# The index lookup of the top-k stage: both POOL subtractions of a head released by DVE's last index operation, which stands behind a weight split

## The reference, cut to what matters

```python
q = (xf @ wq).reshape(T, PEER_HEADS, 2, PEER_KEY_DIM // 2)
s1 = jnp.einsum('thd,kd->thk', q[:, :, 0], kf[0])
s2 = jnp.einsum('thd,kd->thk', q[:, :, 1], kf[1])
v1, i1 = lax.top_k(s1, PEER_TOPK)
v2, i2 = lax.top_k(s2, PEER_TOPK)
cand = (v1[..., :, None] + v2[..., None, :]).reshape(T, PEER_HEADS, PEER_TOPK * PEER_TOPK)
sc, ci = lax.top_k(cand, PEER_TOPK)
e1 = jnp.take_along_axis(i1, ci // PEER_TOPK, axis=-1)
e2 = jnp.take_along_axis(i2, ci % PEER_TOPK, axis=-1)
idx = e1 * PEER_N_KEYS + e2
g = jax.nn.softmax(sc, axis=-1)
```

## Time and profile before

| what | value |
| --- | --- |
| median of three runs | 3645.09 us |
| the profiled execution, its own time | 3633.96 us |
| its span | 3632.2 us |
| PE busy | 3337.1 us (92%) |
| DVE busy | 2583.1 us (71%) |
| ACT busy | 1226.2 us (34%) |
| POOL busy | 942.2 us (26%) |
| mean granted TensorE clock | 0.966 |
| route, first layer | about 440 to 715 us of the span |
| route, second layer | about 2250 to 2525 us |

### The profile page before, as it was taken

The page is one execution under the profiler, slowest core; times in us unless marked ns, Lnnn a source line. Parts: engine busy times, 40 slices in busy tenths (PEclk is TensorE's granted clock), DMA queues, the critical chain, the costliest instruction groups (busy, mean ns, idle before and its releaser), DMA issues. The chain is left out here.

```text
span 3632.2 us, 49494 instructions
## 1 busy us (share of the span) xinstructions
PE 3337.1 (92%) x17238; PEld 2880.9 (79%) x17238; DVE 2583.1 (71%) x5173; ACT 1226.2 (34%) x1704; POOL 942.2 (26%) x648
## 2 busy tenths in 40 slices
PE   7899899798899999999788997998988999999996
PEld 6755589788799999988677555897888999999885
DVE  2364479899688866678723654798996887766786
ACT  2244333333333333333222443333433333333332
POOL 0211001211155544333202110012111554343332
PEclk9999999999899999999999998999999999999998
DMA  9310024456799988789593001244668999887895
GB/s 268 84 42 1 25 83 136 166 220 253 279 344 360 337 277 281 260 291 355 198 261 100 11 1 37 82 139 163 236 233 307 358 355 325 280 275 246 316 352 185
DMA packets 326377, 773.84 MB, mean 213 GB/s; under 512 B 48686, under 2 KB 203822, under 8 KB 291918
## 3 DMA queue, kind: packets, MB, share of 16 engines
q1 hardware_dynamic: 252494, 503.46, 40.3%
q0 software_dynamic: 73728, 268.47, 20.6%
HBM read 689.02 MB, written 90.70 MB: 215 GB/s over the span
## 5 line engine op out<-in xcount | busy, mean ns | idle before, releaser
L219 PE MATMUL o_bank<-v_hi,w_hi 128*128 128x512 f32 x1536 | 599.0, 390 | 12.0 <-DVE w_lo L1426 12.0
L221 PE MATMUL o_bank<-v_hi,w_lo 128*128 128x512 f32 x1536 | 600.0, 391 | 0.0
L220 PE MATMUL o_bank<-v_lo,w_hi 128*128 128x512 f32 x1536 | 599.9, 391 | 0.0
L156 POOL DMA_INDIRECT g_ring<-in_peer_v,g_idx x256 | 398.0, 1555 | 659.4 <-DVE x_sb L174 615.6
L156 POOL DMA_INDIRECT g_ring<-in_peer_u,g_idx x256 | 332.7, 1300 | 727.0 <-DVE g_ring L166 682.6
L1411 DVE TENSOR_TENSOR v_lo<-v_raw,v_hi 128x2048 fp32r<-128x2048 f32 x128 | 293.2, 2290 | 215.5 <-ACT v_hi L1352 215.3
L219 PE MATMUL h_bank<-x_hi,ws_hi 128*128 128x384 f32 x1152 | 387.1, 336 | 4.5 <-PEq L1093 4.5
L221 PE MATMUL h_bank<-x_hi,ws_lo 128*128 128x384 f32 x1152 | 387.0, 336 | 0.0
L220 PE MATMUL h_bank<-x_lo,ws_hi 128*128 128x384 f32 x1152 | 386.6, 336 | 0.0
L1352 ACT CAST v_hi<-v_raw 128x2048 fp32r<-128x2048 f32 x128 | 244.8, 1913 | 387.5 <-PE o_bank L221 349.5
L166 DVE SCALAR_TENSOR_TENSOR g_ring<-g_ring,x_sb 128x1024 f32<-128x1024 f32 x256 | 307.4, 1219 | 81.9 <-DMA g_ring<-in_peer_u,g_idx 81.7
(11 more groups left out here) (181 smaller groups left out, 6208.3 us busy)
## 6 DMA issues: line engine op xcount, KB each, us to landing
ws_raw<-in_uT SPq DMA_DIRECT2D x128, 1024.0 KB
v_raw<-in_peer_v SPq DMA_DIRECT2D x128, 1024.0 KB
gates_T<-gate_stage SPq DMA_DIRECT2D x12, 4096.0 KB, 15.2
g_raw<-gates_T SPq DMA_DIRECT2D x128, 384.0 KB
w_raw<-in_w_in SPq DMA_DIRECT2D x24, 1024.0 KB, 7.6
ws_raw<-hidden_T SPq DMA_DIRECT2D x56, 384.0 KB
ws_raw<-in_peer_wq SPq DMA_DIRECT2D x16, 1024.0 KB
hidden_T<-r_hid SPq DMA_DIRECT2D x32, 384.0 KB, 6.1
```

The lines of the kernel that those rows point to most:

```text
L156: nc.gpsimd.indirect_dma_start(out=tail.ring[n % RING][:, :], out_offset=None, in_=table.rearrange("l e d -> (l e) d"), in_offset=bass.Ind ...
L219: nc.tensor.matmul(out, lh, rh, start=start, stop=False)
L220: nc.tensor.matmul(out, lh, rl, start=False, stop=False)
L221: return nc.tensor.matmul(out, ll, rh, start=False, stop=stop)
```

## The change

DVE's `ab[0]` (L983) no longer raises `placed`; the following step waits on DVE's own chain instead. Split "keys" moves ahead of the last index operation (L991 after, L990 before), which alone raises `placed`, once per head. Both of POOL's subtractions wait for that one increment.

```diff
                 ab = abf[j % 2]
-                nc.vector.scalar_tensor_tensor(ab[:, 0, :, :], shf[:, 1, :, :], -12.0 * RANK, shf[:, 0, :, :],
-                                               ALU.add, ALU.max).then_inc(placed, 1)
-                dve.wait_ge(placed, 2 * j + 1)
+                chain.done(nc.vector.scalar_tensor_tensor(ab[:, 0, :, :], shf[:, 1, :, :], -12.0 * RANK,
+                                                          shf[:, 0, :, :], ALU.add, ALU.max))
+                chain.wait()
                 for f in range(2):
                     chain.done(nc.vector.scalar_tensor_tensor(lin[:, f, :, :], ab[:, 0, :, :], -16.0 + 12.0 * f,
                                                               shf[:, 2, :, :], ALU.mult, ALU.add))
+                after("keys")
                 chain.wait()
                 nc.vector.scalar_tensor_tensor(ab[:, 1, :, :], lin[:, 1, :, :], -48.0 * RANK, lin[:, 0, :, :],
                                                ALU.add, ALU.max).then_inc(placed, 1)
-                after("keys")
...
                 for f in range(2):
-                    pool.wait_ge(placed, 2 * j + f + 1)
+                    pool.wait_ge(placed, j + 1)
                     if j >= 1:
                         pool.wait_ge(looked, 2 * (j - 1) + f + 1)
```

## The result

The changed kernel takes 3621.23 us (median of 7 runs, 3615.86 to 3626.43); the kernel before, in the same comparison, 3641.96 us (7 runs). The ratio is 0.9943, 95% interval 0.9931 to 0.9955: 20.7 us or 0.57% faster. Over all comparisons of this study the change has a mean of 3621.1 us (24 runs) and the kernel before 3640.6 us (87 runs), a gain of 19.5 us, plus or minus 1.8 (95%). The forecast was a gain of 14.4 us, and its range ended 1.5 us above the measured time. The profiled execution of the change took 3615.86 us, its span is 3614.1 us.

The account below looks back on a forecast made before the run. DVE's own time was taken to bound route's heads 3 to 7. Two layers at 7.2 us make 14.4 us, and 3645.09 less that gives 3630.7 us; range 3622.7 to 3640.

Parts of the forecast that it names:

- What bounds route, and the port: Route: DVE's own time sets heads 3 to 7; L987 stands for POOL's subtraction, 1.96 us against 0.22.
- the heads' part: Route, heads 3 to 7: a "keys" head saves 1.86 us of DVE; period near 26.4 us instead of 27.84.
- The rival by which the scan stands: Scan beside POOL's subtractions: a head pays 3.9 us and saves 1.86, giving 3665.5 us; chance 0.05.
- ACT's part as the new limit: Route, "keys" splits wait for ACT's high part; it takes back 1.8 of 9.3 us, head 7 7.52 earlier.
- K: Start of a "keys" split in route; the next head's "half" was to start at K + 12.98.
- The end of the stage: End of route: L1006 stands, goes between POOL's two subtractions and ends 7.3 us earlier; the stage ends 7.2 us earlier.
- the rival of one piece: End of route: POOL runs both subtractions without a gap, 5.4 us a layer instead of 7.2, 3634.3 us; chance 0.15.
- The 0.15 us that I charged to L1017: End of route: the first L1017, due at 701.07, stands 0.15 us until POOL's second subtraction ends.
- I see nothing in gates that would take it back: Gates stage, after route: it begins with the barrier and keeps route's gain of 7.2 us a layer.
- all other stages the same: Stages outside route: no change in length, while route is shorter by 7 us in each layer.
- The sum's base: Whole kernel: the runs' median, 3645.09 us, 11.1 above the profiled execution, from which 14.4 us was taken.
- the range's lower end: Whole kernel: 3622.7 us, from all of DVE's saving (3626.7) and 4 us of spread of medians below.

Follow-up runs that it names:

- the joint release alone: The change with the "keys" split put back behind the last index operation, both POOL subtractions still released by L990: 3626.56 us, ratio 0.9969; again 3627.03 us.
- the moved split alone: The kernel before with the "keys" split ahead of the last index operation, each subtraction released by its own index operation as before: 3635.55 us, ratio 0.999.
- softmax-ahead kernel: The change with head 7's L1004 and L1006 in front of `ab[0]` and the last lookup ahead of the products: 3623.59 and 3625.26 us.

## Why the prediction was wrong

**What bounds route, and the port: right.** L987 fell to 0.22 us, MAX8 and FIND_INDEX8 stayed, and the resource that DVE's two-input operations and POOL's subtractions exclude each other from was the whole reason for the heads' part: the joint release alone brings a head from 27.84 to 26.17 us, the moved split alone to 27.72, both together to 26.29. What the moved split adds lies at the end of the stage, where it leaves one operation standing instead of two. The rival by which the scan stands is out, also with twice the work on POOL.

**ACT's part as the new limit: right for the change, with small errors in size.** "Half" of head 3 starts at 574.92, K + 12.98 to the digit. K of head 7 came 7.76 us earlier counted from head 2's split (139.21 to 131.45 us), forecast 7.52: five heads take 131.45 us and not 131.69.

**The end of the stage: right.** L1006 went between the two subtractions, and the rival of one piece is out; why the one that waits gets its turn there no run shows. The 0.15 us that I charged to L1017 was not paid (it started at 700.19, as POOL ended). With the two small errors a layer gives 7.7 us, not 7.2, 1.0 us in all.

**The step that failed is the one that closed the account at the end of route**: "I see nothing in gates that would take it back", and "all other stages the same". Everything outside of route was put at 0 us; the runs show 4.1 us of gain there (19.5 less 15.4, plus or minus 1.8). I had looked for something that takes the gain back and not for something that adds to it. Gates can add: the experiment that put 1.4 us back at the end of route made its two gates stages 2 us longer, with no later stretch at a granted clock of 1.00. But between the kernel before and the change the gates stages differ by only 0.9 us in the mean, since two of the six of the kernel before are short too; that is 1.8 us of the 4.1, and not clear of their scatter. The difference in project and attend (1.3 us a layer) is smaller than their scatter from profile to profile (431.4 to 440.9 us), and no experiment was aimed at it. So the cause of the 4 us is shown in part at most, and stays open for the rest.

**The sum's base was the second error.** I carried the difference of the three runs shown over to the forecast; their median, 3645.1, lies 4.5 us above the mean of 87 runs, which puts the forecast that much too high. With the better base, 3640.6, the same 14.4 us would have given 3626. The forecast of 3630.7 was 9.5 us too high: 4.5 from the base, 1.0 from route and 4.1 from the other stages. And the range's lower end took the highest gain of route alone with 4 us of scatter, so that a gain of route as forecast, plus a few us from outside, fell out of it.

What stays open as well: whether it is PE's pause itself, or when gates starts against something else, that decides the clock. The softmax-ahead kernel has a still shorter pause, 2.5 us, and gates stages in between, 262.4 to 263.3, so "shorter is better" does not hold.

## What to carry to other kernels

An engine's instruction that is nine times longer in some executions than in others, with the end of the long ones on the end of another engine's, is probably standing for a shared resource. Here the cure cost nothing: the other engine's work could be released a little later, to lie beside operations that leave the resource alone, scans next to which twice the POOL work made nothing longer. Then look for the next limit in the stage (here ACT, for which each later "keys" split waits 0.2 us), and take the base of a forecast from as many runs as there are.

## What the runs showed of the hardware

DVE operations with two tensor inputs in SBUF (L987 1.96 us instead of 0.22, L1006 2.43 instead of 0.69) and a POOL subtraction (3.92 us instead of 1.93 behind a split) excluded each other; also the small copy L1004, with one input, stood (1.92 us instead of 0.18) in the kernel before. When a released subtraction had just ended and another was ready, the DVE operation already waiting went first (0.4 us between POOL's two); in the joint release POOL, waiting behind the split, went before L1004. In each case the one whose row starts first went first. MAX8, MATCH_REPLACE8, FIND_INDEX8, tensor reductions and a reciprocal ran beside POOL at their own length.

Unexpected: where the end of one stage was moved by 1.4 us, the next was 2 us longer in both profiled stages. The clock granted to PE 80 to 240 us later went with it (0.91 to 0.92 throughout, where seven of the eight stages of the change have 1.00 in one or two stretches of 20 us). So a time of this kernel has a part that no sum over its instructions gave here, of the size of the scatter between runs.
